# Second layer's experts: expert weights in one DMA of whole rows a chunk, one pair of experts at a time

## What is computed

```python
def expert_choice_ffn(h, w_router, w_g, w_u, w_d):
    cap = CAPACITY_FACTOR * n // N_EXPERTS            # 64 of 512 tokens
    logits = jnp.einsum('bnd,de->ben', h, w_router)
    gate, idx = lax.top_k(jax.nn.softmax(logits, axis=1), cap)
    xs = h[bi, idx]
    a = jnp.einsum('becd,edf->becf', xs, w_g)
    u = jnp.einsum('becd,edf->becf', xs, w_u)
    y = jnp.einsum('becf,efd->becd', jax.nn.silu(a) * u, w_d)
    return jnp.zeros_like(h).at[bi, idx].add(y * gate[..., None])
```

## Time and profile before

| | |
|---|---|
| median of three runs | 3743.57 us (3741.46 to 3747.7) |
| the profiled execution | 3751.16 us, its span 3749.4 us |
| mean granted TensorE clock | 0.951 of full speed |
| PE / PEld / DVE / ACT busy | 3290.6 / 1628.0 / 886.3 / 622.7 us |
| read from HBM | 547.63 MB, 147 GB/s over the span |
| expert weights, both layers | 768 DMAs of 512 KB, issued by SP |

### The profile page before, as it was taken

One profiled execution on the slowest core, in us unless ns is written; L12 is line 12 of the kernel. 1 busy time (PEld: TensorE's weight loads), 2 busy tenths in 40 slices (PEclk: granted clock), 3 DMA queues, 4 the chain that ended last, 5 costly groups with the idle time before them and its releaser, 6 DMA issues. The chain is left out here.

```text
span 3749.4 us, 36326 instructions
## 1 busy us (share of the span) xinstructions
PE 3290.6 (88%) x14258; PEld 1628.0 (43%) x14258; DVE 886.3 (24%) x1357; ACT 622.7 (17%) x1072; POOL 16.8 (0%) x35
## 2 busy tenths in 40 slices
PE   5887899989995999999987979999778788778978
PEld 3544555545554442433344544444423223233544
DVE  2464611001114001111024562011300010025342
ACT  2162600000002100101021541000201001011141
POOL 1000000000000000000000000000000000000000
PEclk8989999999996999999988989999799999999989
DMA  7100012353510778697851001232188998961200
GB/s 205 45 1 23 1 45 79 124 174 106 169 56 12 262 277 313 238 347 255 313 151 45 1 23 57 58 88 79 34 317 298 356 329 312 358 200 45 68 1 23
DMA packets 381924, 551.94 MB, mean 147 GB/s; under 512 B 65496, under 2 KB 177384, under 8 KB 381640
## 3 DMA queue, kind: packets, MB, share of 16 engines
q1 hardware_dynamic: 379856, 546.53, 42.8%
q0 software_dynamic: 1600, 3.20, 0.3%
q10 hardware_dynamic: 312, 0.05, 0.0%
HBM read 547.63 MB, written 2.10 MB: 147 GB/s over the span
## 5 line engine op out<-in xcount | busy, mean ns | idle before, releaser
L692 PE MATMUL ps<-hT,ring 128*128 128x512 f32 (+1 forms) x2576 | 973.9, 536 | 72.8 <-ACT hT L1132 28.4
L899 PE MATMUL ps<-ring,hT 128*64 128x512 f32 x3072 | 716.8, 604 | 112.3 <-DMA ring<-in_w_e_up 41.2
L692 PEld LDWEIGHTS ps<-hT,ring 128*128 128x128 f32 x2576 | 492.5, 192 | 545.1 <-issue 492.1
L899 PEld LDWEIGHTS ps<-ring,hT 128*64 128x64 f32 x3072 | 202.0, 137 | 604.4 <-issue 401.7
L692 PE MATMUL ps<-obuf,ring 128*128 128x512 f32 (+1 forms) x512 | 198.5, 540 | 2.5 <-DMA ring<-in_w_branch 1.5
L1659 DVE SCALAR_TENSOR_TENSOR xT<-ps,mod,xT 128x512 f32<-128x512 f32 x96 | 63.5, 662 | 535.1 <-PE ps L967 281.1
L905 PE MATMUL ps<-ring,hT 128*32 128x512 f32 x1536 | 184.7, 598 | 0.0
L1132 ACT ACTIVATE prob<-prob,nms 128x768 f32<-128x768 f32 (+5 forms) x224 | 159.2, 711 | 59.9 <-DVE nms L1510 51.8
L1132 ACT ACTIVATE prob<-ps 128x512 f32<-128x512 f32 (+1 forms) x56 | 38.6, 689 | 733.0 <-PE ps L692 733.0
L862 PE MATMUL ps<-obuf,merged 128*128 128x256 f32 x640 | 153.3, 389 | 7.3 <-DVE obuf L1611 4.1
L785 PE MATMUL ps<-con,prob 128*128 128x128 f32 x872 | 135.8, 291 | 26.4 <-ACT prob L1132 25.2
(11 more groups left out here) (185 smaller groups left out, 2292.3 us busy)
## 6 DMA issues: line engine op xcount, KB each, us to landing
ring<-in_w_e_gate SPq DMA_DIRECT2D x256, 512.0 KB, 7.4
ring<-in_w_e_up SPq DMA_DIRECT2D x256, 512.0 KB, 8.2
ring<-in_w_e_down SPq DMA_DIRECT2D x256, 512.0 KB, 7.8
ring<-in_w_in SPq DMA_DIRECT2D x49, 1024.0 KB, 5.2
ring<-in_w_ada SPq DMA_DIRECT2D x48, 1024.0 KB, 11.6
ring<-in_w_in SPq DMA_DIRECT2D x48, 256.0 KB, 5.0
ring<-in_w_branch SPq DMA_DIRECT2D x16, 512.0 KB, 7.3
ring<-in_w_out SPq DMA_DIRECT2D x8, 1024.0 KB, 8.6
```

Of the source, the lines that this page charges most:

```text
L692: mm = pe.matmul(ps[:, b + a:b + e], lhs[:, k, :], rhs[:, k, a:e], start=k == 0, stop=k == nk - 1)
L899: mm = pe.matmul(ps[e * CX:(e + 1) * CX, b + pair * 512:b + (pair + 1) * 512], lhs[:, k, s0:s0 + CX], expert_dst(slot, e)[:, k % 2, :], st ...
```

## The change

For the second layer alone a product is one pair of experts over both column halves, and a chunk is 128 rows of both experts' matrices over all 1024 columns: one DMA of 1 MB whose rows are 4 KB (`expert_loads`), where it was two DMAs with rows of 2 KB. A slot is laid out as two experts by 1024 columns. `pair_product` takes chunk after chunk (`k` of eight) and does four matmuls with each: two halves `h`, two experts `e`; every second chunk raises the semaphore, so slots still come back in pairs. `hid`, `hidT` and `ye` are filled pair by pair: `turn_pair` turns the whole hidden layer of a pair in eight transposes (one job where there were two), and ScalarE copies it in one instruction of 1024 columns (`turned_pair`), as it does the output of a pair (`output_pair`).

The order of a round becomes `eg` 0, `eu` 0, `eg` 1, turn 0, `eu` 1, gather, `ed` 0, turn 1, gather, gather, `ed` 1, last gather, output sums, where the numbers now are pairs. The list of weights follows this order. The first layer keeps its chunks and its order.

```diff
-        SET_JOBS = [("eg", 0), ("eu", 0), ("eg", 1), ("eu", 1), ("in", 0), ("in", 1), ("in", 2), ("ed", 0), ("ed", 1),
-                    ("in", 3), ("out", 0), ("out", 1), ("out", 2), ("out", 3)]
+        SET_JOBS = [[("eg", 0), ("eu", 0), ("eg", 1), ("eu", 1), ("in", 0), ("in", 1), ("in", 2), ("ed", 0), ("ed", 1),
+                     ("in", 3), ("out", 0), ("out", 1), ("out", 2), ("out", 3)],
+                    [("eg", 0), ("eu", 0), ("eg", 1), ("eu", 1), ("in", 0), ("ed", 0), ("in", 1), ("in", 2), ("ed", 1),
+                     ("in", 3), ("out", 0), ("out", 1), ("out", 2), ("out", 3)]]
         PARTS = {"eg": 4, "eu": 4, "ed": 4, "in": 1, "out": 1}
-
-        def turn_jobs(l):
-            return [("gt", 0)] + ([("gt", 1)] if l == 0 else []) + [("ht", n) for n in range(4)]
+        TURN_JOBS = [[("gt", 0), ("gt", 1)] + [("ht", n) for n in range(4)], [("gt", 0), ("ht", 0), ("ht", 1)]]
...
-        ROUND = [(w, half, kk, pair) for w, half in [k for k in SET_JOBS if k[0] in ("eg", "eu", "ed")]
-                 for kk in range(4) for pair in range(2)]
+        WEIGHT_ORDER = [[k for k in js if k[0] in ("eg", "eu", "ed")] for js in SET_JOBS]
+        ROUND = [[(w, half, kk, pair) for w, half in WEIGHT_ORDER[0] for kk in range(4) for pair in range(2)],
+                 [(w, pair, k) for w, pair in WEIGHT_ORDER[1] for k in range(KD)]]
         EXPERT_W = {"eg": w_e_gate, "eu": w_e_up, "ed": w_e_down}
-        assert len(ROUND) % RING == 0
-
-        def expert_dst(s, e):
-            return ring[:, s, e * 1024:(e + 1) * 1024].rearrange("p (k f) -> p k f", k=2)
-
-        def expert_src(l, i, w, half, kk, e):
-
-            at = i * (D * FH) + ((l * E + e) * D + kk * 2 * P) * FH + half * 512
-            return bass.AP(EXPERT_W[w].tensor, at, [[FH, P], [P * FH, 2], [1, 512]])
+        RLEN = len(ROUND[0])
+        assert len(ROUND[1]) == RLEN and RLEN % RING == 0
+
+        def expert_dst(l, s, e):
+
+            if l == 0:
+                return ring[:, s, e * 1024:(e + 1) * 1024].rearrange("p (k f) -> p k f", k=2)
+            return ring[:, s, :].rearrange("p (e f) -> p e f", e=2)
+
+        def expert_loads(l, i, r):
+
+            if l == 0:
+                w, half, kk, pair = ROUND[0][r]
+                return [(e, bass.AP(EXPERT_W[w].tensor, i * (D * FH) + ((2 * pair + e) * D + kk * 2 * P) * FH + half * 512,
+                                    [[FH, P], [P * FH, 2], [1, 512]])) for e in range(2)]
+            w, pair, k = ROUND[1][r]
+            return [(0, bass.AP(EXPERT_W[w].tensor, i * (D * FH) + ((E + 2 * pair) * D + k * P) * FH,
+                                [[FH, P], [D * FH, 2], [1, FH]]))]
...
+                    def pair_product(key, lhs):
+
+                        w, pair = key
+                        b = take(key)
+                        for k in range(KD):
+                            slot, value = chunk_at[LOOPC[1] + ROUND[1].index((w, pair, k))]
+                            pe.wait_ge(w_full[slot], i * (16 * RLEN // RING) + value)
+                            for h in range(2):
+                                for e in range(2):
+                                    s0 = pair * P + e * CX
+                                    mm = pe.matmul(ps[e * CX:(e + 1) * CX, b + h * 512:b + (h + 1) * 512],
+                                                   lhs[:, k, s0:s0 + CX], expert_dst(1, slot, 0)[:, e, h * 512:(h + 1) * 512],
+                                                   start=k == 0, stop=k == KD - 1, tile_position=(0, e * CX))
+                            if k % 2:
+                                done(mm, key)
+
+                    def turn_pair(pair):
+
+                        pe.wait_ge(hm_ready, i * 2 + (1 + pair + half_base))
+                        b = take(("ht", pair))
+                        for k in range(KD):
+                            mm = pe.transpose(ps[:, b + k * P:b + (k + 1) * P], hid[:, pair, k // 4, k % 4 * P:(k % 4 + 1) * P], ident)
+                        done(mm, ("ht", pair))
...
-                    turn_hidden(0)
-                    turn_hidden(1)
-                    experts_product(("eu", 1), xs3)
-                    gather_next(0)
-                    turn_hidden(2)
-                    gather_next(1)
-                    turn_hidden(3)
-                    gather_next(2)
-                    pe.wait_ge(hT_ready, i * 4 + (4 + ROUNDS * 4 * l))
-                    experts_product(("ed", 0), hidT)
-                    experts_product(("ed", 1), hidT)
-                    gather_next(3)
...
+                    else:
+                        pair_product(("eg", 0), xs3)
+                        pair_product(("eu", 0), xs3)
+                        pair_product(("eg", 1), xs3)
+                        turn_pair(0)
+                        pair_product(("eu", 1), xs3)
+                        gather_next(0)
+                        pe.wait_ge(hT_ready, i * HT[1] + (1 + ROUNDS * HT[0]))
+                        pair_product(("ed", 0), hidT)
+                        turn_pair(1)
+                        gather_next(1)
+                        gather_next(2)
+                        pe.wait_ge(hT_ready, i * HT[1] + (2 + ROUNDS * HT[0]))
+                        pair_product(("ed", 1), hidT)
+                        gather_next(3)
...
-                    for n, (w, half, kk, _) in enumerate(ROUND):
-                        t, _, _, f, per = loop_job[l, (w, half)]
-                        chunk_end[LOOPC[l] + r * len(ROUND) + n] = (set_full[t], f - 3 + kk + r * per)
+                    for n, chunk in enumerate(ROUND[l]):
+                        t, _, _, f, per = loop_job[l, chunk[0:2]]
+                        chunk_end[LOOPC[l] + r * RLEN + n] = (set_full[t], f - 3 + (chunk[2] // 2 if l else chunk[2]) + r * per)
...
-                for e in range(2):
-                    src = expert_src(l, i * QUAD, w, half, kk, QUAD * ahead + 2 * pair + e)
-                    sp.dma_start(expert_dst(c % RING, e), src).then_inc(w_full[c % RING], 16)
+                for e, src in expert_loads(l, i * QUAD + QUAD * ahead, n):
+                    sp.dma_start(expert_dst(l, c % RING, e), src).then_inc(w_full[c % RING], 16)
...
+                    def turned_pair(pair):
+                        b = read(("ht", pair))
+                        sc.copy(hidT[:, :, pair * P:(pair + 1) * P],
+                                ps[:, b:b + 1024].rearrange("p (k s) -> p k s", k=KD)).then_inc(hT_ready, 1)
+                        act.wait_ge(hT_ready, i * HT[1] + (1 + pair + ROUNDS * HT[0]))
+                        release(("ht", pair))
+
+                    def output_pair(pair):
+                        b = read(("ed", pair))
+                        sc.copy(ye[:, pair, :], ps[:, b:b + D]).then_inc(y_ready, 1)
+                        act.wait_ge(y_ready, i * 2 + (1 + pair + half_base))
+                        release(("ed", pair))
...
+                        turned_pair(0)
+                        next_in(0)
+                        output_pair(0)
+                        turned_pair(1)
+                        next_in(1)
+                        next_in(2)
+                        output_pair(1)
+                        next_in(3)
```

More of the change, by code:

```diff
@@ L528, in program @@
                 for i in range(ROUNDS):
-                    for r, (w, half, kk, pair) in enumerate(ROUND):
-                        add_chunk(("expert", n, i, r), [(None, expert_src(n, QUAD * i, w, half, kk, 2 * pair + e))
-                                                        for e in range(2)])
+                    for r in range(RLEN):
+                        add_chunk(("expert", n, i, r), [((n, e), src) for e, src in expert_loads(n, QUAD * i, r)])
         def load_params(eng, l):
@@ L584, in program @@
         SEL = {0: 4, 1: 2}
+        HT = {0: 4, 1: 2}
         sel_base = {0: 0, 1: SEL[0] * (ROUNDS + 1)}
@@ L892, in experts_product @@
                             for pair in range(2):
-                                slot, value = chunk_at[LOOPC[l] + ROUND.index((w, half, kk, pair))]
-                                pe.wait_ge(w_full[slot], i * (32 * len(ROUND) // RING) + value)
+                                slot, value = chunk_at[LOOPC[0] + ROUND[0].index((w, half, kk, pair))]
+                                pe.wait_ge(w_full[slot], i * (32 * RLEN // RING) + value)
                                 slots.append(slot)
@@ L1018, in load @@
                     sp.wait_ge(done, value)
-                for e, (at, src) in enumerate(chunks[n]):
-                    if at is None:
-                        dst = expert_dst(slot, e)
+                for at, src in chunks[n]:
+                    if len(at) == 2:
+                        dst = expert_dst(at[0], slot, at[1])
                     else:
@@ L1027, in round_load @@
             def round_load(l, i, n, ahead):
-                c = LOOPC[l] + n + ahead * len(ROUND)
-                w, half, kk, pair = ROUND[n]
+                c = LOOPC[l] + n + ahead * RLEN
```

(38 more changed lines are left out.)

28 lines of the change are left out of this document (20 added, 8 removed).

## The result

The changed kernel takes 3684.76 us (median of four runs, 3680.63 to 3685.31) against 3745.26 us: a ratio of 0.984, 95% interval 0.982 to 0.985. It is 60.5 us faster, where 37.8 were forecast; the low end of the forecast range was 3689. (The median of the kernel before is over four runs here, 3741.46 to 3747.7; the three of them known at the forecast gave 3743.57.)

What follows compares the result with a forecast made beforehand. The second layer's expert stage was taken to wait for weight loads, plus pauses of PE. Rows -28.5, sooner-full ring +4.3 and order -13.6 gave -37.8 us, a median of 3706 us from 3743.6, range 3689 to 3735.

Steps and rivals of the forecast that it cites:

- Rows of 4 KB: Second-layer weight loads: 410 GB/s and 2.56 us a chunk instead of 387 and 2.71, worth -28.5 us.
- The order: PE's round in the second layer: middle pause cut in two, turning pause shortened; 8.6 us lost becomes 5.2, -13.6 us in all.
- the turning pause: PE's pause between `eg` and `eu`: falls from about 2.5 us to 1.04, its 0.7 us loss becoming nothing.
- The first piece: One gather before `ed` of the first pair, 3.6 us long, just under the ring's cover: charged 0.5 us.
- the waits: Two waits added or moved, before `ed` of the first pair and the third gather: hidden, otherwise about 4 us apiece.
- The price of a pause: PE's pauses: free while pause plus 5.5 us stays below 10 us of cover, then one to one plus 1 to 2.
- Why a pause of 11 us costs 8: Ring at PE's pauses: full some 10 us after PE leaves, slots return late, refill slow at 339 GB/s; 7.9 us lost.
- The second piece: Turn and two gathers before `ed` of the second pair, 8.2 us for 11.4: 4.7 us lost, bounds 0 and 7.9.
- Last gather, output sums, gate turns stay: 12.9 us lost: The round's end: its 18.2 us pause keeps costing 12.9 us a round, apart from 0.6 charged elsewhere.
- a faster transfer fills the ring sooner: At each stall the four chunks of cover shrink by 0.6 us: +4.3 us in all.
- restart costs what it costs now: Rival on the stage's pauses: the order helps nothing, only rows do; -24 us, 3719 us, chance 0.12.
- The slower rivals: Ring loads: rows 4 MB apart collide in HBM; 339 GB/s, 3801 us, chance 0.05, or half rate, 4234 us, chance 0.02.

Runs made afterwards that it cites:

- order_2k_two: The changed kernel with each 1 MB chunk fetched by two DMAs of 512 KB with rows of 2 KB, one per column half: 3710.7 us, ratio 0.991.
- before_near: The kernel before, each DMA reading one contiguous 512 KB instead of half rows, so second-layer weights land in wrong places: 3717.1 us, ratio 0.992.
- rows_only: The changed kernel with both `ed` products after all three gathers and both turns, as before: 3691.4 us, ratio 0.986.
- halves_long: halves_far with both `ed` products after three gathers and both turns, one long pause as in rows_only: 3729.8 us, ratio 0.996.
- halves_far: The changed kernel's order and pairs, with chunks of 256 half rows in two 2 KB-row DMAs, all left-half chunks before the right: 3714.9 us, ratio 0.991.

## Why the prediction was right and wrong

- **What bounds it, right.** A stage that waits for transfers, with fixed pauses; 63.1 us of the profiled execution's gain lie in it.
- **Rows of 4 KB, right.** 410 GB/s and 2.56 us a chunk from a line through three row lengths; measured 409 and 2.56. 186 x 0.15 = 28 us. order_2k_two shows that it is the rows' length: with rows of 2 KB the same order runs at 387, and so does before_near, whose rows of 2 KB lie one behind the other. The Trainium skill (DMA: Bandwidth & Descriptors, iDMA fabric, the note on a load stream beside iDMA) has 408.7 GB/s for such a stream alone, and the trace agrees with its 409. The Trainium skill (DMA: Bandwidth & Descriptors, Latency and other measured facts) gives 207 GB/s at a row pitch of 512 KiB from partition to partition and 103 at 4 MiB. That does not reach this pattern: here the partitions lie 4 KB apart, and two pieces 4 MB apart in one DMA run at 409.
- **The order, right, its size partly by luck.** -13.6 us forecast; rows_only's stage is 556.8 us and the change's 543.3: 13.5 (by rounds 3.1 x 4 = 12.4). The medians lie 6.6 apart; in the two profiled executions the stage of the change starts 3.8 us later, and 2.4 us more follow it, neither of which the order touches. But 2.8 of the 13.6 were for the turning pause, which rows_only has already cut, so like for like 10.8 stand against 12.4 to 13.5. And the forecast took 7.9 down to 0.5 + 4.7 where the law gives 4.4 (11.4 - 7) down to 0.9 and the trace 1.0: both prices were over 3 us too dear, and the difference came out nearly right. With half rows (halves_long to halves_far, rounds of 148.17 and 143.74) it is 4.4 us a round. The first piece costs nothing, the waits hide as listed.
- **The price of a pause, wrong, and this is the step that failed.** Under "Why a pause of 11 us costs 8" I took what the trace of before showed, a cover of 10 us, a slow refill, 7.9 and 12.9 us, as properties of the ring, and carried them over to the new chunk. The second piece was priced at 4.7 us and lost 1.0; the first at 0.5 and lost nothing; "Last gather, output sums, gate turns stay: 12.9 us lost" became 11.5; and 1.1 us a round was added because a faster transfer fills the ring sooner. Together 19.2 us a round forecast and 12.6 measured, 6.6 x 4 = 26 us, which is the 25.3 between the 37.8 forecast and the stage's 63.1. The old prices were properties of how the old chunks were read. rows_only has the same pause as before (11.4 us) and the same end, and loses 15.8 us a round where 21.7 were lost. halves_long has these pauses too, with half rows but one pair after the other, and loses 18.1: so of the 5.9 us some 3.6 came with the sequence of the pairs (0.7 of them the turning pause) and 2.3 with whole rows of 4 KB. By rounds the three parts are -28.1 for the rate, -23.6 for the cheaper pauses and -12.4 for the order, -64 against the stage's -63.
- **A hint that I had.** I wrote that the refill was slower than the steady state, and gave no reason. The rival "restart costs what it costs now" asked if the pauses would stay dear; none asked if they would become cheaper, and both the range and the bound of 0 for the second piece left the end of the round, four times 12.9, as it was.
- **The slower rivals, rightly small.** The long rows did not collide: the steady rate is 409 GB/s.

## What to carry to other kernels

Where a stage waits for loads and its pauses are paid, price the pause from the trace by three marks (the last work before it, the time at which the transfers stop, the time at which they return), and say for each what of it belongs to the ring and what to the pattern of the reads. Here a fading end and a slow return of the transfers came from the pattern, and a cheap experiment separated them from the ring: the same kernel reading the same number of bytes from contiguous addresses. Then shorten the longest pause and give slots back one by one; here both together are worth another 16 us. The law P - 7 is that of this ring, these chunks and this rate; another kernel has its own numbers.

## What the runs showed of the hardware

- Rate by row length, in steady stretches: 218 GB/s at 256 bytes, 348 at 1 KB, 387 at 2 KB, 409 at 4 KB; estimated from these, about 9.5 ns a row and 37.6 ns a KB on each of 16 engines.
- The steady rate is blind to what is read (387 GB/s with half rows, whole rows, blocks 512 KB or 4 MB apart); the stops and restarts are not. With half rows of four experts read in turn the transfers fade for some 5 us (206 GB/s over 3 us, then 68 over 4) and return at 354 GB/s over 12 us. With contiguous reads they stop within 1 to 2 us, but for one round's end of three, and return at 383. All kernels that read half rows return slower than they run in the steady part (326 to 379 of 387 GB/s), whether they fade or not.
- One DMA of 1 MB or two of 512 KB a chunk: 1.5 us a round apart at rows of 4 KB, 1.5 us in the medians, which their spread does not separate.
